# The low half of the MLP up weights: a negated copy and an accumulating load in place of a subtraction

## What is computed

```
D_MODEL = 1024;  D_FF = 4 * D_MODEL;  DEPTH = 2
def sq_relu_mlp(h, w_up, w_down):
    return jnp.square(jax.nn.relu(h @ w_up)) @ w_down
for layer in range(DEPTH):
    h = h + mixer(...)                                   # sparse attention, then latent attention
    h = h + sq_relu_mlp(rms_norm(h, mlp_norm[layer]), mlp_w_up[layer], mlp_w_down[layer])
```

## Time and profile before

| | us |
|---|---|
| median of three runs | 1127.31 |
| lowest, highest | 1125.93, 1128.98 |
| the profiled execution | 1128.73 |
| its span, first to last instruction | 1127.0 |
| TensorE busy in the span | 1103.6 (98%) |
| VectorE busy | 770.0 (68%) |
| ScalarE busy | 601.4 (53%) |
| GpSimd busy | 138.4 (12%) |

### The profile page before, as it was taken

The page is one execution under the profiler, slowest core; times in us unless marked ns, Lnnn a source line. Parts: engine busy times, 40 slices in busy tenths (PEclk is TensorE's granted clock), DMA queues, the critical chain, the costliest instruction groups (busy, mean ns, idle before and its releaser), DMA issues.

```text
span 1127.0 us, 17838 instructions
## 1 busy us (share of the span) xinstructions
PE 1103.6 (98%) x7003; PEld 979.4 (87%) x7003; DVE 770.0 (68%) x1077; ACT 601.4 (53%) x778; POOL 138.4 (12%) x104
## 2 busy tenths in 40 slices
PE   8999999999998999999999999999999999999996
PEld 7868888888887888888889999898899989999995
DVE  5864665656668646555656878566588578988885
ACT  5574644444688554444446546455545357555552
POOL 3632200000275240000030000000000002000001
PEclk9999999999999999999999999999999999999998
DMA  9735465556412236556545553446643456654631
GB/s 344 236 115 113 159 216 189 186 191 225 169 53 104 75 117 226 196 187 197 189 156 187 195 169 129 149 149 216 215 155 127 163 211 225 213 176 170 223 131 38
DMA packets 138785, 194.00 MB, mean 172 GB/s; under 512 B 7147, under 2 KB 112840, under 8 KB 138716
## 3 DMA queue, kind: packets, MB, share of 16 engines
q1 hardware_dynamic: 126796, 181.92, 47.7%
q10 hardware_dynamic: 11312, 11.05, 3.5%
q0 software_dynamic: 608, 0.08, 0.0%
HBM read 191.90 MB, written 6.37 MB: 176 GB/s over the span
## 4 chain that ended last, share of the span: by engine, by line
PE 80%; DVE 8%; ACT 7%; issue 3%; DMA 0%; POOL 0%; ACTq 0%; DVEq 0%; POOLq 0%
PE psum L619 19%; PE psum L620 19%; PE psum L621 19%; PE psum L828 9%; PE psum L829 5%; ACT arena L1692 4%; ACT whi L1706 2%; PE psum L707 2%; DVE wlo L2322 2%; PE psum L1358 1%; PE psum L1385 1%; DVE psum L2781 1%; DVE arena L2848 1%; PE psum L737 1%; PE psum L888 0%
## 5 line engine op out<-in xcount | busy, mean ns | idle before, releaser
L2322 DVE TENSOR_TENSOR wlo<-raw,whi 128x2048 fp32r<-128x2048 f32 (+2 forms) x135 | 304.7, 2264 | 127.6 <-ACT whi L1706 126.5
L1706 ACT ACTIVATE whi<-raw 128x2048 fp32r<-128x2048 f32 (+3 forms) x153 | 285.1, 1872 | 182.8 <-PE psum L621 128.0
L619 PE MATMUL psum<-xA,whi 128*128 128x256 f32 x840 | 239.3, 285 | 0.0
L620 PE MATMUL psum<-xA,whi 128*128 128x256 f32 x840 | 237.6, 283 | 0.0
L621 PE MATMUL psum<-xA,wlo 128*128 128x256 f32 x840 | 237.6, 283 | 0.0
L828 PE MATMUL psum<-xA,whi 128*128 128x512 f32 x512 | 181.9, 398 | 0.0
L1675 POOL TENSOR_TENSOR wlo<-raw,whi 128x288 fp32r<-128x288 f32 (+3 forms) x43 | 81.9, 1930 | 755.2 <-ACT whi L1706 755.1
L619 PEld LDWEIGHTS psum<-xA,whi 128*128 128x128 f32 x840 | 160.3, 191 | 3.2 <-issue 2.1
L620 PEld LDWEIGHTS psum<-xA,whi 128*128 128x128 f32 x840 | 160.4, 191 | 1.1
L621 PEld LDWEIGHTS psum<-xA,wlo 128*128 128x128 f32 x840 | 160.3, 191 | 0.1
L829 PE MATMUL psum<-xA,wlo 128*128 128x256 f32 x512 | 143.6, 280 | 0.0
(11 more groups left out here) (305 smaller groups left out, 1697.6 us busy)
## 6 DMA issues: line engine op xcount, KB each, us to landing
raw<-in_w_in SPq DMA_DIRECT2D x42, 1024.0 KB, 4.8
raw<-in_mlp_w_up SPq DMA_DIRECT2D x32, 1024.0 KB, 5.3
raw<-in_mlp_w_down SPq DMA_DIRECT2D x32, 1024.0 KB, 4.8
raw<-in_w_gate SPq DMA_DIRECT2D x11, 1024.0 KB, 5.0
raw<-in_w_up SPq DMA_DIRECT2D x11, 1024.0 KB, 6.3
down_raw<-in_w_down SPq DMA_DIRECT2D x6, 1024.0 KB, 8.1
arena<-in_w_down SPq DMA_DIRECT2D x5, 1024.0 KB, 7.8
raw<-in_b_w_o SPq DMA_DIRECT2D x4, 1024.0 KB, 5.0
```

Of the source, the lines that this page charges most:

```text
L619: nc.tensor.matmul(out, lh, rh, start=start, stop=False, skip_group_check=skip)
L620: nc.tensor.matmul(out, lh, rl, start=False, stop=False, skip_group_check=skip)
L1706: nc.scalar.activation(whi[split_of[c]][:, 0:n], raw_bufs[raw_of[c]][:, 0:n], ACT.Copy).then_inc(hi_sem, 1)
L2322: V.tensor_tensor(wlo[split_of[c]][:, 0:n], raw_bufs[raw_of[c]][:, 0:n], f(whi[split_of[c]][:, 0:n]), ALU.subtract).then_inc(lo_sem["dve"], 1)
```

## The change

For up chunks u2 to u15 and for the last down chunk d15 of each MLP the field `lo` becomes "dma". Such a chunk gets its low part in three steps. ScalarE, right after the high part, makes a second pass over the landing buffer with scale -1 into `wlo`; rounding is symmetric, so this is the negated high part. GpSimd then waits for it and for its own last accumulating load, and issues a load of the same weights from memory into `wlo` that adds to what is there: -high + value. TensorE waits for that load's semaphore, which counts 16 for each. The landing buffer counts as free once the negated copy is made. VectorE's loop loses the second `low_part`. The chunk d15 is in the change because in its turn it stands where up chunks stand otherwise.

```
-                lo = "pool" if x < 2 else "dve"
                 if kind == "u":
-                    cols(f"mlp{i}.u{j}", up[i], STEP * j, STEP, lo=lo)
+                    cols(f"mlp{i}.u{j}", up[i], STEP * j, STEP, lo="pool" if j < 2 else "dma")
                 else:
-                    rows(f"mlp{i}.d{j}", down[i], 2 * j, 2, D, lo=lo)
+                    rows(f"mlp{i}.d{j}", down[i], 2 * j, 2, D, lo="dma" if j == n - 1 else "dve")
...
-                low_n[chunk["lo"]] += 1
+                low_n[chunk["lo"]] += 16 if chunk["lo"] == "dma" else 1
...
+                elif chunks[users[0]]["lo"] == "dma":
+                    semaphore, values = negated, [low[x] // 16 for x in users]
...
+                if chunks[c]["lo"] == "dma":
+                    pool.wait_ge(negated, low[c] // 16)
+                    if low[c] > 16:
+                        pool.wait_ge(lo_sem["dma"], low[c] - 16)
+                    (_, k, n, _, _, src), = chunks[c]["loads"]
+                    pool.dma_start(wlo[split_of[c]][:, 0:k * n].rearrange("p (k n) -> p k n", n=n), src,
+                                   accum_op=ALU.add).then_inc(lo_sem["dma"], 16)
+                    continue
...
                 nc.scalar.activation(whi[split_of[c]][:, 0:n], raw_bufs[raw_of[c]][:, 0:n], ACT.Copy).then_inc(hi_sem, 1)
+                if chunks[c]["lo"] == "dma":
+                    nc.scalar.activation(wlo[split_of[c]][:, 0:n], raw_bufs[raw_of[c]][:, 0:n], ACT.Copy,
+                                         scale=-1.0).then_inc(negated, 1)
...
                     V.tensor_tensor(xC[:, 1024 * j3 + 512:1024 * j3 + 1024], sqr_buf,
                                     f(xC[:, 1024 * j3:1024 * j3 + 512]), ALU.subtract).then_inc(hlo_done, 1)
-                    if splits:
-                        low_part(*splits[1])
```

More of the change, by code:

```diff
@@ L292, in program @@
         hi_sem = sem("weight_high_ready")
-        lo_sem = {"pool": sem("weight_low_ready_pool"), "dve": sem("weight_low_ready_dve")}
+        lo_sem = {"pool": sem("weight_low_ready_pool"), "dve": sem("weight_low_ready_dve"),
+                  "dma": sem("weight_low_ready_dma")}
+        negated = sem("weight_high_negated")
         landed, count = [0] * NC, [0] * (N_RAW + 8)
@@ L296, in program @@
         first_raws = (0, 1, 4, 5, 6, 0, 1, 4, 5, 6, 4)
-        low, low_n = [0] * NC, {"pool": 0, "dve": 0}
+        low, low_n = [0] * NC, {"pool": 0, "dve": 0, "dma": 0}
         high, raw_of, split_of = [0] * NC, [0] * NC, [None] * NC
@@ L2500, in step @@
                                     f(xC[:, 1024 * j3:1024 * j3 + 512]), ALU.subtract).then_inc(hlo_done, 1)
-                    if splits:
-                        low_part(*splits[1])
                 def static(p):
                     a = c0 + 1 + 2 * p
-                    step(b0 + p + 1, b0 + p + 1, b0 + p if b0 + p else None, p % 2, p % 3, [(c, high[c]) for c in (a + 1, a + 2)] if p < NM - 1 else None)
+                    step(b0 + p + 1, b0 + p + 1, b0 + p if b0 + p else None, p % 2, p % 3, [(a + 1, high[a + 1])] if p < NM - 1 else None)
                 for p in range(3):
@@ L2513, in mlp @@
                         v = along([b0 + p + 1 for p in ps_], r)
-                        step(v, v, along([b0 + p for p in ps_], r), (q + 1) % 2, q % 3, [(c0 + 1 + 2 * ps_[0] + w, along([high[c0 + 1 + 2 * p + w] for p in ps_], r))
-                                       for w in (1, 2)])
+                        step(v, v, along([b0 + p for p in ps_], r), (q + 1) % 2, q % 3, [(c0 + 2 + 2 * ps_[0], along([high[c0 + 2 + 2 * p] for p in ps_], r))])
                 static(NM - 1)
```

## The result

| | before | after |
|---|---|---|
| median, us | 1128.0 | 1266.3 |
| ratio | | 1.123, 95% interval 1.122 to 1.125 |
| span of the profiled execution, us | 1127.0 | 1264.8 |
| TensorE busy, us | 1103.6 | 1132.0 |
| VectorE busy, us | 770.0 | 701.8 |

The kernel is 138 us slower. Of all executions behind the tables of this document one alone fell out of line, 2786 us for the variant with pieces of 4 KiB, and it is left out of that variant's median.

The account below looks back on a forecast made before the run. TensorE, with no gap in the loop, was taken to bound the kernel; 30 chunks at 2.8 us make 84, plus 5 for the starts, on 1128.7 gives 1217.7, against the median 1216 us; range 1127 to 1330 us.

Parts of the forecast that it names:

- What bounds the kernel: In the MLP loop TensorE is busy 115.50 of 115.5 us; at most 0.22 us to win at each MLP's start.
- ScalarE's pass at no cost: In the MLP loop, ScalarE's second pass raises its load from 4.8 to 6.7 us of 11.1; claimed free.
- X: Time from an up chunk's negated part to the landed sum: 12.6 us, 5.6 more than the slack.
- moving: Term of X, the accumulating load's time on the DMA engines: 6.8 us, taken as twice the plain load's 3.4.
- company: Term of X: SP's next up load, starting with the accumulation, brings 3.4 us of work to the same engines.
- issue and fixed part: Terms of X: 0.5 us from GpSimd's issue until the engines start, 1.9 us fixed part of a landing.
- the slack: From an up chunk's negated part at 206.31 to TensorE's need at 213.43: 7.0 us after a 0.1 us hop.
- heavy rival: Moving 10.2 us or slow descriptors, down load included: X 19.1 us, GpSimd's one transfer at a time, some 1370 us; chance 0.20.
- twice a plain load: Choice for moving in X: 6.8 us, between 3.4 and 10.2, since accumulating takes two reads for one write.
- The recurrence: In the MLP loop, a stall and the one before together make 5.6 us, so a turn loses 2.8 on average.
- The ends: First such chunk of each MLP has only 4.5 us and loses 8.1; 5 us added for both MLPs together.
- "hidden" rival: The transfer lands before TensorE's up product wants it, 5.8 us against 7.0; time stays 1127 us; chance 0.10.

## Why the prediction was right, and where it was short

**What bounds the kernel.** Right: there was nothing to win. VectorE's 68 us less bought no time, and the stage behind the MLPs kept its 539.0 us.

**ScalarE's pass at no cost.** Right, and shown by the run in which only this pass was added.

**X = 12.6 us.** It was 13.9. By its terms: moving 6.8 us was taken and 6.8 measured; company 3.4 taken, 3.9 measured; issue and fixed part 2.4 taken, 2.8 left over. These make 13.5, the landing of the loads on the path, and 0.3 us pass between the negated part and the issue, where the slack had 0.1 for a hop. The company was made up differently than argued: the sum counted SP's next up load and kept the down load for the heavy rival, but with a turn of 11.1 us the down load follows the up load by 6.1 us, well inside a transfer of 12. The value "twice a plain load" was a choice between 3.4 and 10.2 without a row; the run without the addition shows that it came out right as a sum of 3.9 for the way over GpSimd and 2.9 for the addition, and not as 3.4 doubled, so there is luck in it.

**The recurrence, (X - 7.0) / 2 a turn.** Right in form. With the measured X it gives 3.4 us a turn in the changed kernel; with it and the slow clock 4.3, as measured (a turn of 15.4). The quarter-size run meets the threshold, the run with one load in three shows the missing half: 9.4 us a load, where a whole overrun of 6.9 and a slow clock of 1.8 make 8.7.

**The term that was missing: TensorE's clock.** A stall of over 6 us is followed by four microseconds at the lower level, 1.8 us a pair, 0.9 a turn, some 25 of the 139 us. TensorE's busy time, 28.4 us longer for the same matmuls, and the run with filled waits agree. The prediction took TensorE's products at their length in the earlier trace rows and did not ask what idleness does to it; in the kernel before the loop has none.

**The ends.** 5 us were taken for both starts; start and seam together gave back 11 when eased, and the burst of SP's loads at the seam was not seen, though SP's order stands in the code. It shows in the traces: the last up load of the first MLP takes 16.8 us to land in the changed kernel, 16.3 without the addition (where TensorE waits 9.4 us for it), 11.4 at quarter size, and 6.5 once the burst goes out later. The loop's excess, 28 x 4.3 = 120 us, and the ends make up the 138.

**The forecast was 1216 us, the result 1266.** Of the 50 us, 0.65 us a turn come from X (20 us with all 30 chunks), 0.9 from the clock (27), and the rest, some 3, from the ends. The "hidden" rival failed on company and on the addition, each of which alone moves X across 7.0 us; the plain load on GpSimd's queue needs 8.1 us beside SP's up load and would not have been hidden either. The "heavy" rival was out: the engines' time is 6.8 us and not 10.2, and one transfer at a time did not set the turn. One piece of it came true, the down load that falls into the transfer.

No variant here beats the kernel before. Its loop has no gap on TensorE, and the smallest accumulating load tried already costs 13 us.

## What to carry to other kernels

Before moving work from an idle engine to a transfer, compare the transfer's whole latency, with whatever starts beside it, to the slack of that one chunk, not engine shares to each other: VectorE had 4.5 us of air in a turn that the change did not need, and the transfer had 7.0 us where it needed 13.9. Company is not a fixed price: a longer transfer also meets the load after next, so shortening it paid more here than the time cut from it (5.4 us of landing for 2.9 of the engines and 0.7 of issue). When a buffer ring feeds a busy TensorE, an overrun costs half of itself a turn if all chunks overrun and all of itself if few do, and stalls of six or seven microseconds bring the lower clock on top. When an experiment replaces a step, check which buffers it holds longer than the change does; otherwise it measures its own cycle.

## What the runs showed of the hardware

An accumulating load of 1 MiB in 1 KiB pieces from GpSimd's queue takes 6.8 to 7.0 us of all sixteen engines, the same load without the addition 3.9, SP's plain load 3.4, and in pieces of 4 KiB the accumulating one takes 5.6. GpSimd needs 1.55 us to issue it (1024 pieces), 0.88 without the addition, 1.20 with 256 pieces. Beside an up load and a down load of SP the accumulating load landed 13.5 us after issue, beside the up load and with the down load 9.2 us behind it 11.3, with the up load cut to an eighth 9.6. After 6.6 us without work TensorE ran 4 us at a granted clock of 0.52; filling the gap with throwaway matmuls kept it at 1.00 in the loop and took 25 us off the time of the other matmuls, and the whole program became 30 us quicker.
